# Expert layers: the scatter of a pair issued ahead of the gather for the pair three on

## What is computed

```python
grp = jnp.argmax(group_score, axis=-1)                 # one of 4 groups of 8 experts
_, loc = lax.top_k(sel_in, EXPERT_TOPK)                # two experts in it
wts = wts / jnp.sum(wts, axis=-1, keepdims=True)
hg = jax.nn.silu(einsum('nd,edf->nef', xt, w_gate)) * einsum('nd,edf->nef', xt, w_up)
out = out + einsum('nef,efd->nd', hg * gate, w_down)   # 32 experts, inner width 256
x = layer_norm(alpha * x + out, g, b)
```

## Time and profile before

| | us |
|---|---|
| median of three runs | 1170.09 |
| lowest and highest | 1162.45, 1173.85 |
| the profiled execution | 1163.89 |
| its span in the profile | 1160.5 |
| TensorE busy | 1063.1 (92%) |
| VectorE busy | 455.1 (39%) |
| ScalarE busy | 234.7 (20%) |
| GpSimd busy | 131.2 (11%) |
| mean DMA rate | 269 GB/s |

### The profile page before, as it was taken

How to read it: one execution, slowest core, us unless ns; L and a number is a source line. 1 busy time by engine, 2 the same in 40 slices (tenths; PEclk the granted TensorE clock), 3 DMA queues, 4 the chain that set the end, 5 groups by cost and what they waited for, 6 DMA issues and landing times. The chain is left out here.

```text
span 1160.5 us, 13972 instructions
## 1 busy us (share of the span) xinstructions
PE 1063.1 (92%) x4918; PEld 544.3 (47%) x4918; DVE 455.1 (39%) x1167; ACT 234.7 (20%) x552; POOL 131.2 (11%) x197
## 2 busy tenths in 40 slices
PE   8899999998999989998888799899899899998883
PEld 6577767674334543333333466455554433333321
DVE  0788655546655552211111833222114522211117
ACT  0211223115001311111111313322113121111112
POOL 0000104100000011111110022320000111111010
PEclk9899999999999999999998799999999999999997
DMA  7129511205354989999998765563258599999993
GB/s 283 66 107 363 210 73 45 108 30 223 145 225 156 414 348 425 425 420 425 423 422 352 278 221 174 171 220 125 110 235 336 176 419 425 420 424 421 421 370 117
DMA packets 54913, 312.01 MB, mean 269 GB/s; under 512 B 13058, under 2 KB 13954, under 8 KB 34242
## 3 DMA queue, kind: packets, MB, share of 16 engines
q1 hardware_dynamic: 43426, 298.04, 64.3%
q0 software_dynamic: 11264, 12.61, 3.3%
q10 hardware_dynamic: 160, 0.52, 0.1%
HBM read 300.61 MB, written 33.59 MB: 288 GB/s over the span
## 5 line engine op out<-in xcount | busy, mean ns | idle before, releaser
L1402 PE MATMUL ps<-ring,xsT 128*64 128x512 f32 x704 | 160.9, 610 | 22.1 <-DMA ring<-in_experts 17.8
L1757 DVE TENSOR_TENSOR work<-work,ps 128x256 f32<-128x256 f32 x32 | 13.5, 421 | 268.6 <-ACT work L1486 268.6
L434 PE MATMUL ps<-XT,ring 128*128 128x320 f32 x384 | 108.1, 446 | 9.8 <-DMA ring<-in_w_in 5.3
L1402 PEld LDWEIGHTS ps<-ring,xsT 128*64 128x64 f32 x704 | 54.6, 140 | 125.4 <-issue 117.7
L434 PEld LDWEIGHTS ps<-XT,ring 128*128 128x128 f32 x384 | 75.3, 197 | 41.8 <-issue 7.5
L1402 PE MATMUL ps<-hi,xsT 128*64 128x512 f32 x320 | 75.7, 628 | 8.6 <-DMA hi<-in_experts 8.6
L1429 PE MATMUL ps<-ring,hT 128*64 128x512 f32 x352 | 80.4, 598 | 1.5 <-ACT hT L1490 0.9
L366 PE MATMUL ps<-XT,ring 128*128 128x320 f32 x256 | 76.9, 445 | 0.0
L1551 POOL DMA_INDIRECT y_dram<-ys,index x32 | 32.4, 1012 | 376.3 <-DVE ys L1789 333.7
L1327 PE MATMUL ps<-C 128*128 128x512 f32 x140 | 71.6, 631 | 0.6 <-PEq L836 0.3
L1543 POOL DMA_INDIRECT XT<-x_dram,index x32 | 32.8, 1024 | 314.0 <-DVE index L1686 282.3
(11 more groups left out here) (358 smaller groups left out, 1390.4 us busy)
## 6 DMA issues: line engine op xcount, KB each, us to landing
ring<-in_experts SPq DMA_DIRECT2D x36, 2048.0 KB, 24.5
ring<-in_experts SPq DMA_DIRECT2D x60, 1024.0 KB, 22.2
hi<-in_experts SPq DMA_DIRECT2D x20, 2048.0 KB, 24.6
hi<-in_experts SPq DMA_DIRECT2D x20, 1024.0 KB, 27.5
ring<-in_w_in SPq DMA_DIRECT2D x9, 2048.0 KB, 12.4
ring<-in_latent SPq DMA_DIRECT2D x60, 256.0 KB, 4.3
ring<-in_w_out SPq DMA_DIRECT2D x4, 2048.0 KB, 7.4
ring<-in_state SPq DMA_DIRECT2D x4, 1024.0 KB, 7.8
```

The lines of the kernel that those rows point to most:

```text
L434: return pe.matmul(ps[:, q, 0:TOK], ring[:, u, k * 512 + q * P:k * 512 + (q + 1) * P], XT[:, k, :], start=(k == 0), stop=(k == KD - 1))
L1402: mm = pe.matmul(ps[e * SLOTS:(e + 1) * SLOTS, GU[p], :].rearrange("p (g f) -> p g f", g=2), xsT[:, p, k, e * SLOTS:(e + 1) * SLOTS], w[:, ...
```

## The change

Inside GpSimd's loop the gather for pair j + 3 moves from the front of an iteration to its end, behind the scatter of pair j. The three gathers ahead of the loop, the waits inside `gather` and `scatter`, and all other engines' lists are unchanged. The block for the last pair, which has no gather in its iteration, stays.

```diff
                         for j in range(3):
                             gather(j)
                         for j in range(PAIRS):
-                            if j + 3 < PAIRS:
-                                gather(j + 3)
                             if j == LAST:
                                 pool.wait_ge(ys_out[0], PER_WINDOW * w + 16 * (PAIRS // 2))
                                 pool.wait_ge(ys_out[1], PER_WINDOW * w + 16 * (PAIRS // 2 - 1))
@@
                                 for got in got_in:
                                     pool.wait_ge(got, 16)
                             scatter(j)
+                            if j + 3 < PAIRS:
+                                gather(j + 3)
                         pool.reg_mov(n_windows, load_windows(pool))
```

## The result

The changed kernel is slower: a median of 1239.81 us over four runs (1230.03 to 1242.71) against 1169.09 us (1162.45 to 1173.85), a ratio of 1.0603 with a 95% interval of 1.0568 to 1.0639. The forecast was 1222 us, with 1190 to 1265 as its range. The profiled execution took 1242.71 us.

The account below looks back on a forecast made before the run. DMA's expert weight loads were taken to bound the kernel, TensorE close behind. Late gathers add 31.2 us up to T(12), less 2 at the layer's end: 29.2 a layer, 58.4 for two, on 1163.9 gives 1222; range 1190 to 1265.

Parts of the forecast that it names:

- slack: TensorE in the expert layers: DMA set the end before, so TensorE had some time to spare; no size given.
- T(j): The end of down(j) in a layer, marked by SP's down loads; T(0) to T(12) was forecast at 198.1 us against 166.9.
- closed loop: Down ends, scatter, gather, landing, turn, down: one round takes 7.7 us + L, against 13.0 if nothing is late.
- L: Landing time of a gather: 2.9 us with DMA nearly idle, 7.3 beside a weight burst, 10.5 to 14.8 in full stream.
- pairs 4 to 10: Middle of each layer: DMA load and landing hold each other, 16.1 us a pair, 112.7 for seven.
- the clock: TensorE's clock can fall after waits: 1.7 us added to pairs 1 and 2, half given back in pairs 4 to 10.
- pairs 11 and 12: Late in each layer SP issues only down loads: L of 7.3 and 6.3, pairs of 15 + 14 us.
- The end of the layer: Behind T(12): with the queue empty the last weights land sooner, gate_up(15) starts near T(12) + 21, -2 us a layer.
- Hidden: Rival: DMA empties once TensorE is late and gathers land early enough; 1164 to 1170 us, chance 0.10.
- Faster: Rival: gather(3) leaves the first weight bursts, GpSimd's queue is shorter; at most 0.4 us a layer, 1163 us, chance 0.03.
- Mild: Rival: L is 7.3 once the queue thins, pairs 1 to 10 at the DMA floor; +15.6 a layer, 1195 us, chance 0.12.
- Heavy: Rival: L stays at the full stream's shortest, seven pairs at 18.7 us; +18.2 more a layer, 1259 us, chance 0.15.

Follow-up runs that it names:

- lean twin: The kernel before with gate and up loads of experts 8 to 29 cut to a quarter, so part of the weights is left out; 1130.11 us, ratio 0.9704.
- e1: The changed kernel, but gather(j+3) waits for the copies of down(j) itself and goes out ahead of scatter(j); 1192.35 us, ratio 1.0227 to the kernel before.
- e3: The changed kernel with gate and up loads of experts 8 to 29 cut to a quarter; 1144.50 us, beside 1167.07 for the kernel before.
- e7: The changed kernel with turn(j+2) moved behind down(j), the copies in the same order; 1190.99 us, ratio 1.0186 to the kernel before.
- e2: The kernel before with only gather(3) moved behind scatter(0) in each layer; 1170.43 us, ratio 1.0021.
- e6: The changed kernel with 2 idle matmuls (1.9 us) in front of turn(3) to turn(15); 1221.26 us, ratio 1.0441 to the kernel before.
- e8: The kernel before with each gather held until gate_up two pairs ahead of its turn is done, some 5.3 us later; 1169.39 us, ratio 0.9998.
- e5: The changed kernel with 4 idle matmuls (3.4 us) in front of turn(3) to turn(15); 1225.32 us, ratio 1.0464 to the kernel before.

## Why the prediction was right, and where it was off

**The bound and the slack.** Right. DMA set the end, and waits for weights vanished with the change. I called TensorE's slack "some" and never sized it. The lean twin sizes it: 17.3 and 16.4 us a layer. It could have been read from before: in layer 1 the waits for weights ahead of gate_up(10) to (15) are 1.38, 2.61, 0.80, 2.71, 1.08 and 4.21 us, and gate_up(11) and (13) ran 3.1 us longer together than at full speed, 15.9 us up to the start of gate_up(15). (The gate_ups that the earlier trace rows and the prediction call (9), (10) and (13) are (10), (11) and (14), since gate_up(j + 2) is the one that follows T(j); the 62.6 us between two of them are four pairs all the same.)

**The move itself.** Right: issue at T + 2.82, turn(3) reached 8.24 behind T(0), a wait there, and a closed loop. e1, e3 and e7 each open or shorten it at another place and the time follows; in e2 only one gather is late and it doesn't close.

**The landing L.** The level held and the pair-by-pair course did not. Pair 1 was given 20.4 us and took 21.8 and 20.7. Pair 2 was given 22.0 and took 14.3 and 19.2, as its gather landed in 6.8 and 8.8 us and not in 12.6: it looks as if one long pair thins the queue enough, where I had it full for two. Pair 3 was given 14 and took 20.2 and 14.2. That the first three add up to 56.3 and 54.0 against 56.4 is luck, in layer 0 above all. The mean of pairs 4 to 10 was to settle a little above DMA's 15.65: I took 16.1 and it is 16.6 in layer 0 and 16.9 in layer 1. The L behind my 16.1 is about 8, and the gathers of the twelve pairs landed in 8.3 and 8.1 us in the mean, between the 7.3 and 10.5 of the rows. What I had not seen is that it alternates. As I read it, after a long pair that pair's gate and up loads are through when the next gather goes out, and it lands in 5.5 to 7 us; that makes a short pair of 13 to 14.5, behind which the next gather meets the loads and takes 8 to 11.5, and its pair 18 to 22 (in layer 1 pairs 1 and 2, and 8 and 9, are long in a row). The landings and pairs are measured, that reason is not tested. In layer 1 the SP rows give 20.7, 19.2, 14.2, 19.9, 14.3, 19.8, 13.7, 18.4, 19.0, 13.2, 19.2 and 13.1.

**The term that was mis-sized** is, as far as the runs show, the clock. I charged 1.7 us to the first two pairs and, net of a shorter landing, 0.45 to each of the seven in the middle. In the long pairs the wait is 2.8 to 6 us, and each such wait was followed by a fall. Three windows of 2 us in layer 1 behind the wait that ended at 1011.68 (the granted clock is the third number from the end):

```profile
1011.00:1013.00 2.00, 1.32 (x6) 1.32 (x7) 0.00 (x0) 0.17 (x1) 0.00 (x0) 0.50 0.99 418
...
1013.00:1015.00 2.00, 2.00 (x8) 0.78 (x8) 1.31 (x4) 1.33 (x4) 0.00 (x0) 0.50 1.00 426
...
1015.00:1017.00 2.00, 2.00 (x6) 0.47 (x4) 0.05 (x1) 0.00 (x0) 0.00 (x0) 0.50 1.01 434
```

The clock fell while TensorE stood still for 3.2 us. It is granted at 0.50, the lower level of 1.2 GHz, for some 6 us, and turn and down take 1.97 + 5.63 us in place of 1.04 + 3.65. In turn and down such a fall costs 1.4 to 3.1 us, and up to T(12) there are six in layer 0 and seven in layer 1: 15.5 and 16.6 us. My 1.7 in each of nine pairs would be 15.3, so the gross was about right; what I let a shorter landing give back, 8.7 of it, was too much, and the two falls of pair 11 (2.6 and 1.4 us) had no term at all. How much is really given back no run isolates. e6, with most falls gone, comes nearest: its pairs 4 to 10 take 113.8 and 113.3 us, where I forecast 112.7 and the changed kernel took 116.2 and 118.3, and its pairs 11 and 12 take 30.6 and 30.2, against 29 and 33.6 and 32.3. So of the 8.1 and 8.9 us that the pairs from 4 on ran over the forecast, 5.4 and 7.1 are gone in e6, although 1.9 us of idle matmuls were added to each pair; the changed rhythm may have a part in it. The rest is in pairs 11 and 12, where I had L at 7.3 and 6.3: pair 11 is a long one, with a landing of 10.2 us in both layers, and that the loads thin out there shows in pair 12 alone (5.6 and 5.5 us).

| term, us per layer | forecast | layer 0 | layer 1 |
|---|---|---|---|
| pairs 1 to 3 | 56.4 | 56.3 | 54.0 |
| pairs 4 to 10 | 112.7 | 116.2 | 118.3 |
| pairs 11 and 12 | 29 | 33.6 | 32.3 |
| T(0) to T(12) over before | +31.2 | +39.3 | +37.8 |
| the end behind T(12) | -2 | -3.2 | -3.2 |
| in all | +29.2 | +36.1 | +34.5 |

**The end of the layer.** Right in sign. gate_up(15) starts 1.5 and 1.4 us sooner behind T(12), and with the weights there it also runs in 7.04 us and not in 8.8 or 8.9, which I had left out.

**The rivals.** Hidden needed a mean landing of 6.2 us; it is near 8 and only every second gather is at 6. Faster needed the stall to be absent. Mild needed pairs 1 to 10 at DMA's 15.65 and took no account of the clock; pairs 4 to 10 run at 16.6 and 16.9. Heavy supposed that L stays at the shortest of the full stream; DMA at a share of 0.90 shows why it doesn't. The rule of the Trainium skill in "DMA: Bandwidth & Descriptors", section "Anatomy of one DMA — SWDGE (gpsimd) path", would have given an estimated 2.4 us: the trace comes near it with DMA idle (2.9 us at the least) and not beside the stream. The same page's section "Queues, rings and completion order" says that a DMA engine serves its queues in turn, a packet at a time. That fits what e3 shows, a landing that falls from 8.8 and 8.3 to 6.4 and 5.6 us with smaller weight loads beside it; but no run here varied the packets by themselves, so this cause of the long landing is argued and not shown.

The range held the time, and the forecast of +58.4 us was 17% short of the 70.7 measured.

## What to carry to other kernels

Before moving an issue behind another on a queue, compare what is left to its consumer with the landing time in the same load, not with the landing of an idle DMA: here 18.4 us became 5.4, against landings of 8 to 14 at the median. If the late consumer stands in front of the work that releases the next issue, the loop closes and every turn pays; a single late transfer (e2) cost nothing, because the engine had waits elsewhere to give up, and neither did transfers that went out later and still fitted (e8). Size those waits first (here 17 us a layer) and then charge each new wait on TensorE with what its clock loses behind it, here 1.4 to 3.1 us behind each of the fifteen longer waits.

## What the runs showed of the hardware

- In the changed kernel all fifteen waits of 2.4 us and more at the turns were followed by a slowed turn, and the granted clock behind the one looked at was 0.50; none of the eight shorter waits, 0.4 to 1.4 us, was. It isn't the length of the wait alone: in e5 one of 3.06 us and in e1 one of 2.71 us were followed by a turn of 1.09 and a down of 3.65 us, as at the full clock, and in e1 one of 1.78 us by a down of 5.34. A kernel with 3.4 us of idle matmuls in every pair (e5) was 14.5 us faster than the changed kernel, which has waits in their place (1225.32 and 1239.81, beside 1169.05 and 1169.09 for the kernel before).
- The landing of a gather issued by GpSimd depends on the weight loads beside it: at the median 8.8 and 8.3 us in the changed kernel, and 6.4 and 5.6 with most of those loads cut to a quarter (e3). Within one layer of the changed kernel it ran from 5.5 to 11.5 us.
- In e1, with the gather first, the scatter behind it landed in 10.3 and 10.1 us at the median (layer 0, layer 1); with the scatter first it was 7.8 in layer 1. The gather itself landed in 9.0 and 8.6 us when first and in 8.8 and 8.3 behind the scatter. DMA was fuller in e1 (0.97 and 0.96 against 0.90), so this doesn't show what the order alone does.
- A matmul of 512 float32 columns over all 128 by 128 takes TensorE 0.86 us in a row of four, in two records (eight records from 1013.96 to 1017.39 in e5).
